# One table for the small parameters, an opening stripe in two loads and halves, and short warming products

## What is computed

```python
def rmsnorm(x, g):
    xf = x.astype(jnp.float32)
    y = xf * lax.rsqrt(jnp.mean(xf * xf, axis=-1, keepdims=True) + EPS)
    return (y * g.astype(jnp.float32)).astype(x.dtype)

# run_trunk, first lines of the layer
h = rmsnorm(x, g_mix[l])
proj = h @ w_in[l]                                   # 1024 x 2560
qr, fr, ir, gr, u = jnp.split(proj, [512, 1024, 1536, 2048], axis=-1)
```

## Time and profile before

| | |
|---|---|
| median of three runs | 1428.45 us (1428.28 to 1429.18) |
| the profiled execution, its own time | 1430.4 us |
| span of its instructions in the trace | 1428.7 us |
| PE busy | 1404.9 us, 98% of the span |

### The profile page before, as it was taken

The page is one execution under the profiler, slowest core; times in us unless marked ns, Lnnn a source line. Parts: engine busy times, 40 slices in busy tenths (PEclk is TensorE's granted clock), DMA queues, the critical chain, the costliest instruction groups (busy, mean ns, idle before and its releaser), DMA issues.

```text
span 1428.7 us, 25494 instructions
## 1 busy us (share of the span) xinstructions
PE 1404.9 (98%) x9965; PEld 1364.1 (95%) x9965; DVE 886.8 (62%) x1350; ACT 420.3 (29%) x632; POOL 577.5 (40%) x457
## 2 busy tenths in 40 slices
PE   8999999999999999999999999999999999999997
PEld 7999999989999987799999999999999999999996
DVE  4425577878753257757995766676667658633335
ACT  6231434470021135510052222322222222311111
POOL 1232246135532010124563787778777610000163
PEclk9999999999999999999999999999999999999998
DMA  9412211101162274611132122212221142523113
GB/s 296 127 45 59 75 31 36 41 23 45 50 185 61 73 252 171 211 45 45 44 89 75 62 87 88 74 61 87 88 74 61 58 156 74 171 90 113 33 45 119
DMA packets 163567, 129.19 MB, mean 90 GB/s; under 512 B 11532, under 2 KB 148748, under 8 KB 163363
## 3 DMA queue, kind: packets, MB, share of 16 engines
q1 hardware_dynamic: 163499, 128.25, 29.0%
HBM read 107.88 MB, written 20.58 MB: 90 GB/s over the span
## 4 chain that ended last, share of the span: by engine, by line
PE 65%; POOL 12%; issue 10%; DVE 7%; ACT 2%; DMA 2%; SPq 1%; POOLq 0%; DVEq 0%; ACTq 0%
PE pm L2247 17%; PE pm L2249 17%; PE pm L2248 17%; POOL gb L998 2%; POOL raw_c L980 2%; POOL raw L980 2%; PE pm L2518 2%; PE pm L2520 2%; PE pm L2519 2%; POOL sum L987 2%; POOL sum L985 2%; DMA xt<-in_x_prompt 1%; DMA sk<-in_cache_k_cols 1%; DVE w_lo L1544 1%; POOL raw L992 1%
## 5 line engine op out<-in xcount | busy, mean ns | idle before, releaser
L2247 PE MATMUL pm<-x_hi,w_hi 128*128 128x344 f32 x960 | 310.6, 323 | 0.8 <-DVE gb L1611 0.8
L2249 PE MATMUL pm<-x_hi,w_lo 128*128 128x344 f32 x960 | 306.6, 319 | 0.0
L2248 PE MATMUL pm<-x_lo,w_hi 128*128 128x344 f32 x960 | 306.6, 319 | 0.0
L1083 ACT ACTIVATE w_hi<-raw 128x1024 fp32r<-128x1024 f32 x88 | 93.3, 1060 | 531.3 <-PE pm L2249 455.3
L2247 PEld LDWEIGHTS pm<-x_hi,w_hi 128*128 128x128 f32 x960 | 180.4, 188 | 2.7 <-issue 2.0
L2248 PEld LDWEIGHTS pm<-x_lo,w_hi 128*128 128x128 f32 x960 | 180.4, 188 | 0.2
L2249 PEld LDWEIGHTS pm<-x_hi,w_lo 128*128 128x128 f32 x960 | 180.4, 188 | 0.0
L1544 DVE TENSOR_TENSOR w_lo<-raw,w_hi 128x1024 fp32r<-128x1024 f32 x79 | 113.4, 1435 | 11.2 <-ACT w_hi L1083 11.2
L831 POOL TENSOR_TENSOR raw<-raw,gains 128x1024 f32<-128x1024 f32 x32 | 64.6, 2025 | 128.6 <-DMA raw<-in_w_in 82.0
L2094 DVE TENSOR_TENSOR gb<-gb,ga 128x1032 f32<-128x1032 f32 x19 | 53.0, 2788 | 89.9 <-POOL gb L998 89.9
L2205 DVE TENSOR_TENSOR acc<-pm,acc 128x344 f32<-128x344 f32 x66 | 33.9, 515 | 112.2 <-PE pm L2249 112.0
(11 more groups left out here) (366 smaller groups left out, 3973.5 us busy)
## 6 DMA issues: line engine op xcount, KB each, us to landing
raw<-in_w_ffn_in SPq DMA_DIRECT2D x24, 512.0 KB, 4.5
sg_raw<-s_rows SPq DMA_DIRECT2D x22, 516.0 KB, 5.0
s_rows<-gb SPq DMA_DIRECT2D x21, 516.0 KB, 2.7
raw<-in_w_in SPq DMA_DIRECT2D x20, 512.0 KB, 3.8
raw_c<-in_w_ffn_in SPq DMA_DIRECT2D x20, 512.0 KB, 4.9
sk<-in_cache_k_cols SPq DMA_DIRECT2D x16, 512.0 KB, 6.9
raw<-in_w_out SPq DMA_DIRECT2D x8, 512.0 KB, 3.6
raw<-in_w_cq SPq DMA_DIRECT2D x8, 512.0 KB, 3.6
```

Of the source, the lines that this page charges most:

```text
L1083: act.activation(w_hi[s][:, :, :], src, ACT.Copy).then_inc(hi_made, 1)
L2247: pe.matmul(out, w_hi[s][:, k, :], hi[:, k, x0:x0 + cols], start=(k == 0), stop=False)
L2248: pe.matmul(out, w_hi[s][:, k, :], lo[:, k, x0:x0 + cols], start=False, stop=False)
L2249: last = pe.matmul(out, w_lo[s][:, k, :], hi[:, k, x0:x0 + cols], start=False, stop=(k == kb - 1))
```

## The change

- **One table.** The host packs the seven small vectors into one array of 128 rows of 48 numbers; one DMA brings it into `table`, ahead of everything else. `gains`, `gmem`, `lbt`, `hnorm` and `pscale` become views of it. The seven loads of single numbers and their semaphores are gone. The table takes 32 bytes less in each partition than the five tiles did, and what is allocated behind it moves down by that.
- **Opening stripe in two loads.** Stripe one comes as blocks 0-3 and blocks 4-7, each with a semaphore of its own.
- **Two parts of x ahead of stripe two.** SP issues stripe two behind the second part of x by columns.
- **Halves.** ACT's and DVE's work on stripes one and two goes by halves of four blocks, with semaphores `first_halves` (high) and `first_rests` (low); a group of the first chunk starts on the first half of the low weights. ACT's order is stripe one, x parts 0 and 1, half of stripe two, x part 2, the other half.
- **Warming.** Twenty products of 128 columns, `ones` by `ones`, in place of seven of 512 columns, `ones` by `keep`; they wait for `ones` (the third setup step) and not for `keep` (the ninth).

```diff
-        gains = put("gains", [P, 3, KB])
-        gmem = put("gmem", [P, KB])
-        lbt = put("lbt", [P, 2, H])
+        table = put("table", [P, 48])
+        gains = table[:, 0:3 * KB].rearrange("p (n k) -> p n k", n=3)
+        gmem = table[:, 24:32]
+        lbt = table[:, 32:40].rearrange("p (n h) -> p n h", n=2)
+        hnorm, pscale = table[:, 40:44], table[:, 44:48]
...
-        WARM = 7
+        WARM = 20
...
-            sp.dma_start(gains[:, 0, :], t["g_mix"].rearrange("(k p) -> p k", p=P),
-                         allow_slow_non_contiguous=True).then_inc(gmix_in, 16)
-            load_stripe(phases[0], 0, 0, False)
-            load_stripe(phases[0], 0, 1, False)
+            first_w = t["w_in"].rearrange("(k p) n -> p k n", p=P)[:, :, 4 * P:5 * P]
+            sp.dma_start(table[:, :], t["table"]).then_inc(table_in, 16)
+            sp.dma_start(raw[:, 0, 0:KP, :], first_w[:, 0:KP, :]).then_inc(first_in, 16)
+            sp.dma_start(raw[:, 0, KP:KB, :], first_w[:, KP:KB, :]).then_inc(raw_in[0], 16)
             for n in range(9):
                 c, (k0, k1) = n // 3, PARTS[n % 3]
                 sp.dma_start(xc[:, c, k0:k1, :], t["x_cols"][c, :, k0:k1, :]).then_inc(x_in[n], 16)
+                if n == 1:
+                    load_stripe(phases[0], 0, 1, False)
...
             load_stripe(phases[0], 1, 1)
-            sp.dma_start(gains[:, 1, :], t["g_cross"].rearrange("(k p) -> p k", p=P),
-                         allow_slow_non_contiguous=True).then_inc(const_in, 16)
...
             def first_hi(s, k0=0, k1=KB):
 
-                act.wait_ge(gmix_in, 16)
-                act.wait_ge(raw_in[s], 16)
+                act.wait_ge(table_in, 16)
+                act.wait_ge(*((first_in, 16) if (s, k0) == (0, 0) else (raw_in[s], 16)))
...
-            first_hi(0)
-            first_hi(1, 0, KB // 2)
-            for n in range(3):
-                x_round(n)
-            first_hi(1, KB // 2, KB)
+            first_hi(0, 0, KP)
+            first_hi(0, KP, KB)
+            x_round(0)
+            x_round(1)
+            first_hi(1, 0, KP)
+            x_round(2)
+            first_hi(1, KP, KB)
...
-                dve.wait_ge(const_in, 16 * 6)
+                dve.wait_ge(table_in, 16)
...
-            first_lo(0)
+            first_lo(0, 0, KP)
+            first_lo(0, KP, KB)
             for n in range(3):
                 x_rest(n)
-            first_lo(1)
+            first_lo(1, 0, KP)
+            first_lo(1, KP, KB)
...
-                pe.wait_ge(lo_made, s + 1)
+                pe.wait_ge(*((first_rests, s + 1) if c == 0 else (lo_made, s + 1)))
...
+                    if (c, k) == (0, KP):
+                        pe.wait_ge(lo_made, s + 1)
...
-            pe.wait_ge(setup, 9)
+            pe.wait_ge(setup, 3)
             for _ in range(WARM):
-                pe.matmul(bank[7][:, :], ones[:, :], keep[:, :], start=True, stop=True)
+                pe.matmul(bank[7][:, 0:P], ones[:, :], ones[:, :], start=True, stop=True)
```

More of the change, by code:

```diff
@@ L128, in hybrid_layer @@
         rb = put("rb", [P, T])
-        gains = put("gains", [P, 3, KB])
-        gmem = put("gmem", [P, KB])
-        lbt = put("lbt", [P, 2, H])
+        table = put("table", [P, 48])
[3 more added lines that the diff above has]
+        hnorm, pscale = table[:, 40:44], table[:, 44:48]
         lbw = put("lbw", [P, 4, H])
         omlb = put("omlb", [P, H])
-        hnorm = put("hnorm", [P, H])
-        pscale = put("pscale", [P, H])
         ss = put("ss", [P, 16])
@@ L280, in hybrid_layer @@
         evac = sem("evac")
-        const_in = sem("const_in")
-        gmix_in = sem("gmix_in")
+        first_in = sem("first_in")
+        first_halves = sem("first_halves")
+        first_rests = sem("first_rests")
+        table_in = sem("table_in")
         setup = sem("setup")
@@ L1042, in _ @@
                 if p is phases[0]:
-                    pool.wait_ge(gmix_in, 16)
+                    pool.wait_ge(table_in, 16)
                 ahead = p.name in ("cq", "in0")
@@ L1092, in first_hi @@
             def first_hi(s, k0=0, k1=KB):
-                act.wait_ge(gmix_in, 16)
-                act.wait_ge(raw_in[s], 16)
+                act.wait_ge(table_in, 16)
+                act.wait_ge(*((first_in, 16) if (s, k0) == (0, 0) else (raw_in[s], 16)))
                 for k in range(k0, k1):
                     last = act.activation(w_hi[s][:, k, :], raw[:, s, k, :], ACT.Copy, scale=gains[:, 0, k:k + 1])
-                if k1 == KB:
-                    last.then_inc(hi_made, 1)
+                last.then_inc(*((hi_made, 1) if k1 == KB else (first_halves, 1)))
             def x_square(n):
@@ L1552, in x_rest, with first_lo @@
                                   ALU.subtract).then_inc(x_split, 1)
-            def first_lo(s):
-                dve.wait_ge(hi_made, s + 1)
-                for k in range(KB):
+            def first_lo(s, k0, k1):
+                dve.wait_ge(table_in, 16)
+                dve.wait_ge(*((hi_made, s + 1) if k1 == KB else (first_halves, s + 1)))
+                for k in range(k0, k1):
                     last = dve.scalar_tensor_tensor(w_lo[s][:, k, :], raw[:, s, k, :], gains[:, 0, k:k + 1],
                                                     w_hi[s][:, k, :].bitcast(F32), ALU.mult, ALU.subtract)
-                last.then_inc(lo_made, 1)
+                last.then_inc(*((lo_made, 1) if k1 == KB else (first_rests, 1)))
             def spread_factors(c):
@@ L2786 @@
     t["cache_k_cols"] = nc.dram_tensor("in_cache_k_cols", a.shape, mybir.dt.from_np(a.dtype), kind="ExternalInput").ap()
+    g = [inputs[n].reshape(KB, P).T for n in ("g_mix", "g_cross", "g_ffn", "g_mem")]
+    g += [inputs[n].reshape(-1, P).T for n in ("hgrn_lb", "hgrn_norm", "pool_scale")]
+    arrays["in_table"] = a = np.ascontiguousarray(np.concatenate(g, axis=1))
+    t["table"] = nc.dram_tensor("in_table", a.shape, mybir.dt.from_np(a.dtype), kind="ExternalInput").ap()
     t["s_rows"] = nc.dram_tensor("s_rows", (P, FB, T), F32).ap()
```

## The result

The change makes the kernel slower by 5.4 us (0.34%), outside the forecast's range and on its wrong side. One run of all that are reported here, of e14, took 3544.53 us in the slower state of the chip and is left out of that kernel's ratio.

A forecast was written before the change was run, and what follows sets the result against it. PE was taken to bound the kernel, busy 1404.9 of 1428.7 us; its 1.65 us gain would end in waiting for row blocks, so only their 0.45 counted: 1428.45 to 1428.0 us, range 1425.3 to 1430.2.

The forecast's parts named there:

- Two paths, the later one decides: Until the third stripe starts at 37.59 us, PE's groups run beside the second three row blocks' landing and processing; the later decides.
- The table, 0.45 us: In the opening's DMA queue, one table load lands the row blocks 0.45 us earlier, at 31.22 and not 31.67.
- x ahead of stripe two: In the opening, without stripe two's 1.8 us (293 GB/s) ahead, part 1 of x lands at 7.95 and not 10.23.
- PE's 1.65 us: PE's own path in the opening gains 1.65 us: its six groups end at 33.5 and not 35.16.
- Warming: Ahead of PE's first group, the short products end at 8.0, before x allows that group at 9.1.
- The longer wait and the clock: Rival, chance 0.06: PE's idle time at the spread of row factors grows to 2.8 us, the clock falls: 1430.1.
- 0.45 us reaches the end: Behind the opening PE runs at its own pace, so the third stripe's gain of 0.45 us reaches the kernel's end.
- POOL in front of DVE: Rival, chance 0.11: at the third stripe's low part POOL comes first and DVE waits up to 1.75 us: 1429.75.

The follow-up runs named there:

- e14: e9 with twenty warming products of 176 columns in place of seven of 512; 1428.56 us.
- e10: The changed kernel, with ACT splitting the third stripe ahead of the second three squares and PE spreading later factors behind that stripe's first two groups; 1429.90 us.
- e12: e10 with 32 short warming products in place of twenty; 1430.23 us.
- e2: The kernel before with its tiles moved down by 32 bytes, all else as before; 1429.14 us.
- e4: The kernel before with the one table load in place of the seven small loads, at the old addresses; 1428.19 us.
- e6: The changed kernel with the old warming, seven products of 512 columns; 1432.33 us.
- e7: The changed kernel with both the old order of the loads and the old warming; 1429.82 us.
- e5: The changed kernel with the old order of the loads, stripe two ahead of all x; 1431.84 us.
- e3: The changed kernel with DVE waiting for POOL's eight low parts ahead of the last group of products; 1436.42 us.
- e9: e4 with ACT splitting the third stripe ahead of the second three squares and PE spreading later factors behind that stripe's first two groups; 1427.89 us.

## Why the prediction was wrong

- **Two paths, the later one decides: right**, and it is what the change fell over. e10 and e12 take the row blocks off the path and get a part of the loss back. But the sum stood on one execution, in which the row blocks' path ended 1.8 us behind PE's and which was late; in e2 and e4 the two paths end within 0.3 us of each other.
- **The table, 0.45 us: right** in e4 (0.64), but the row blocks of after did not land at 31.2.
- **x ahead of stripe two: the first step that failed.** I moved x forward by stripe two's 1.8 us at 293 GB/s, as if the queue would deliver the same stream in another order. It delivered 236 and 295 GB/s from 4 to 8 us where it had 271 and 357, and part 0 came whole at 9.06 and not at 6.7. "From there on all x is ahead of it as before" took the row blocks' place in the queue for granted: their path was forecast as untouched but for the table, landing at 31.2. They landed at 33.0 in the mean of the eight profiles with the new order, against 31.1 in the old, and e6, with the old warming, shows what the new order costs without the new warming, 2.7 us. The two loads of stripe one had a part in the late x (e7 and e5 above).
- **PE's 1.65 us: failed with it.** The first product came at 11.55 and not at 9.1. By that the halves of the low weights, which were ready, had nothing to feed; e7 shows them at zero.
- **Warming: the size right** (end at 8.43 for 8.0), **the consequence missed.** With x at 9.1 the pause would have been 1.1 us; with x unmoved it was 3.1, and the clock fell to 0.50 for 3.41 us. I had priced warming that ends too late and not one that ends too early.
- **The longer wait and the clock: the right mechanism with a chance of 0.06.** It was priced as the work of a PE that comes early. Here the wait came from row blocks that come late, so that the wait and the fall add: 1430.1 took only the fall.
- **"0.45 us reaches the end": failed.** Behind the opening I took PE's pace as fixed. The race near 317 us costs 2.3 us of wait (2.95 for 0.24 and 0.39) and by the estimate 1.7 of clock where it goes wrong (3.4 in all, by how far after and e12 fall behind e4 between 309 and 496 us): in two of the seven profiles with twenty or more warming products (e3 left aside), in none of the eight with seven. That they differ by chance alone is not excluded, and how often it happens in runs without a profile isn't known. And 52 instructions at the start moved every later load of code; near 590 us PE waits for the value cache in all eight profiles with twenty or more products, 0.1 to 1.7 us, and in none with seven.
- **POOL in front of DVE: not there** in the opening: the low part that I feared for takes its usual time in after, 1.23 us (the line below). DVE and POOL got in each other's way in a place that I had not looked at.

```profile
36.31 1.23 DVE L1537 TENSOR_TENSOR w_lo<-raw,w_hi 128x1024 fp32r<-128x1024 f32 x1 [1.95 <-ACT w_hi L1075]
```

So the step that failed is the one that moved x ahead of stripe two at 293 GB/s and left the rest of the queue and PE's pace behind the opening as they were. Open are three things: why the queue delivers less and later in the new order (no row shows the single engines, and the new order was never run with one load of stripe one), what tips the race, and why after's median lies as far above before's as it does: the parts above are read from one execution of each kernel.

## What to carry to other kernels

Taking work off the path that ends first doesn't only gain nothing: it can lengthen a wait on the other path, and a longer wait of PE can cost clock besides. Before loads are reordered for the sake of the first, look at what lands last behind them, and take the consumer off that landing first. Count instructions as a possible cost of their own: here 52 more at the start shifted the loading of code through the rest of the program, and a load near 590 us came later by it.

## What the runs showed of the hardware

- The granted clock fell to 0.50, 1.2 GHz, behind PE's idle times of 2.2, 2.4, 2.9, 3.0, 3.1 and 3.4 us, and didn't behind 1.4 and 1.5 at the spread, nor behind 2.0 (e10) and 2.4 (e5) between warming and first products. So the length of the pause alone doesn't settle it. A fall lasted 3.41 us, in e3 twice that.
- Where POOL's low part starts some 50 to 60 ns behind the first of a row of eight short DVE operations (near 317 us), either the two engines take turns (DVE's operations take 1.23 us and not 0.5, POOL's 1.22 and not 0.93), or POOL's takes 4.22 us, until DVE's eight are done (after, e12). The starts don't tell the two apart.
- Code came in 16 KB pieces of 0.9 to 2.1 us each on the engines that move data, 47 of them in most runs. That it is mostly TensorE's is inferred: 52 more TensorE instructions moved the fourth piece from 103 to 77 us (e9, e14). An issue of SP for the value cache that met one took 0.9 to 1.6 us and not 0.43.
